# Five projections of the second tile moved into the first tile's attention, and one gathered row in six weighed on VectorE

## The chip, the cores and the metric

The kernel runs on one core of one Trainium2 chip. The metric is the device time of one execution in microseconds. Of the kernel before, three runs gave 1480.18, 1478.48 and 1479.16 us, median 1479.16 us.

## The reference, cut to what matters

256 tokens of width 1024 go through two blocks in float32. The first (projections, a short convolution, a gated delta rule, a convolutional feed-forward) is not touched. The second block works on two tiles of 128 tokens:

```python
# per token: modulated norm, then columns of w_in_2: qa 512 | tok 440 (latent, rope key, index rows) | qb 512 | kb 512 | vb 512 | forget 8
score = sum_h relu(iq_h . ik) * iw_h ; sel = top_k(score, 64)          # branch A: sparse attention over a latent
p_a   = softmax(where(selected and causal, q_lat . latent + q_rope . k_rope))
p_b   = softmax(causal(qb . kb * scale + cum_q - cum_k))               # branch B: forgetting attention
x = x + gate1 * (concat(norm(o_a), norm(o_b)) @ w_out)
h2 = modulated_norm(x)
for head in range(8):                                                   # product keys: 16 of 128 x 128 experts
    expert, g = top16(q1 . keys1, q2 . keys2)
wgt = softmax(g) * gelu(h2 . u[expert])                                 # 128 experts for each token
x = x + gate2 * sum_k wgt_k * v[expert_k]
```

Rows u and v of an expert (1024 numbers each) lie beside each other in HBM, 8 KB together.

## The kernel before

Every engine has its program written out by hand, and semaphores join them. The second block starts where L1033 stands: TensorE ends the feed-forward of the first, and then does tile 0's projections, attention, output projection and expert queries without anything beside them (L1049 to L1130). Tile 1 of the block shares its weights, but is computed later.

**Gathers.** A set is one expert for each of a tile's 128 tokens: one indirect DMA (L2397, GpSimd) brings 128 rows of 8 KB, 1.05 MB, to a slot of SBUF. There are 256 sets, 128 for a tile. `GATHER` says which slot each set takes and which set had it before; there are 7 slots, three more from set 82 and two more from set 116 (`JOIN`). For each set VectorE multiplies the u half by h2 and sums (L2215, "the dot"), ScalarE takes the gelu (L1431), GpSimd lays the weights on a diagonal (L2369), and TensorE multiplies the diagonal by the v half into two PSUM banks (L1027, four instructions of the trace a set). GpSimd may issue the next gather into a slot when TensorE has used it (L2396). The first gather needs the experts of tile 0's first head, which VectorE finds in 17 steps (`route`, L2101 to L2163).

**Ticks.** All of tile 1's work runs between the sets. `until(tick)` on an engine first does that engine's part of the sets up to the tick (TensorE up to tick - 2, ScalarE tick - 1), so the order on each engine is fixed by numbers: tile 1's index rows at tick 3, its projections from tick 6 to 31, its attention from tick 32 on in steps of 4 ticks (`att_tick`), its output projection from 76 (`T_WOUT`), its expert queries from 93 (`T_QUERY`).

**Weights.** Blocks of 2 MB stream through three buffers `wr`, each loaded by SyncE as soon as the block that had the buffer is used: in this part tok, qb, kb, qa, vb, two of w_out, two of w_peer_q (`weight_blocks`). The gathers take over these buffers, so tile 1 can't use the same weights later: they are loaded a second time, in 18 pieces of 0.9 or 1 MB, two at a time in two buffers of their own (`piece`, L531): pieces 0 and 1 before the block starts, each other as the piece two before it is used. TensorE waits for them in `landed_piece`. Tile 1's tok projection (L865) is the one that already stands ahead of the gathers, between tile 0's output projection (L1099, L1104) and the transposes of its expert input (L848).

PSUM banks 0 to 3 go round in the order of the table in `pair_table`; a step waits until the bank of its turn is empty (`claim_bank`). Each engine is in order: what waits holds back all behind it.

Lines that the prediction names: L857, L865 and L881 projections; L890 forget logits; L898 and L848 transposes; L908 index scores; L949 attention logits; L1099 and L1104 output projection of tile 0; L998 expert queries; L2001 and the line behind it one round of the selection of 64 keys; L2022 masks of logits; L1899 in the first block a multiply and add over 1024 columns by VectorE.

## Time and profile before

| | us |
|---|---|
| median of three runs | 1479.16 |
| the profiled execution | 1486.33 |
| its span | 1484.4 |
| PE (TensorE) busy | 1354.0 |
| DVE (VectorE) busy | 841.1 |
| POOL (GpSimd) busy | 429.6 |
| ACT (ScalarE) busy | 292.7 |
| moved by DMA | 424.52 MB, mean 286 GB/s |
| of these by the gathers' queue | 268.48 MB |

The page's chain that ended last gives PE 54%, DMA 26%, issue 7%, POOL 7% of the span. A chain is followed back from the end: where it runs over a DMA, the gather's landing was what came last. Busy times are averages over stages with different limits, so the rows below are cut by stage. In a timeline row the columns are: start and duration in us, engine, line, instruction, what it writes and reads, shape, count; in brackets how long the engine sat idle before it and what ended that.

### The profile page before, as it was taken

How to read it: one execution, taken by the hardware profiler on the slowest of the kernel's cores; microseconds unless marked ns; L12 is line 12 of the kernel's file. 1: busy time of each engine (PE TensorE's matmuls, PEld its weight loads, DVE VectorE, ACT ScalarE, POOL GpSimd, SP SyncE). 2: the span in 40 equal slices, each digit the busy share in tenths (PEclk: the TensorE clock that was granted, in tenths of full speed). 3: DMA queues.
4: the chain of work that ended last, by engine and by line, in shares of the span. 5: the costliest groups of instructions: out<-in, count | busy, mean ns of one | idle time of the engine just before them, and what ended most of it. 6: DMA issues, size and time to landing. Idle time of an engine off the chain costs nothing.

```text
span 1484.4 us, 14879 instructions
## 1 busy us (share of the span) xinstructions
PE 1354.0 (91%) x5314; PEld 872.2 (59%) x5314; DVE 841.1 (57%) x1997; ACT 292.7 (20%) x690; POOL 429.6 (29%) x545
## 2 busy tenths in 40 slices
PE   7999999999999999999988989998989778778776
PEld 6887888898767777667566554444543222222222
DVE  3558451235127667524256567776766767666654
ACT  2023101031010000114423214541221112111101
POOL 0002000120101000000004544564557555655551
PEclk9999999999999999999898998999999999999999
DMA  8343633311557888537339998999999999999995
GB/s 293 115 170 114 227 114 113 120 51 57 171 186 282 309 297 293 204 127 284 113 114 364 423 422 332 395 421 424 424 424 425 425 425 425 425 426 424 425 425 229
DMA packets 119193, 424.52 MB, mean 286 GB/s; under 512 B 10642, under 2 KB 34632, under 8 KB 84176
## 3 DMA queue, kind: packets, MB, share of 16 engines
q0 software_dynamic: 36896, 268.48, 43.7%
q1 hardware_dynamic: 82224, 155.09, 29.0%
q8 instruction: 43, 0.70, 0.2%
q14 instruction: 30, 0.25, 0.0%
HBM read 422.48 MB, written 1.06 MB: 285 GB/s over the span
## 4 chain that ended last, share of the span: by engine, by line
PE 54%; DMA 26%; issue 7%; POOL 7%; ACT 3%; DVE 3%; SPq 0%; POOLq 0%; DVEq 0%; ACTq 0%
PE psum L560 30%; DMA arena<-peer_uv,arena 15%; DMA wr<-peer_uv,arena 7%; PE psum L811 4%; PE psum L1027 3%; POOL wr L2397 3%; POOL arena L2369 2%; DMA xc<-peer_uv,arena 2%; PE psum L787 2%; PE psum L881 1%; PE psum L857 1%; POOL arena L2397 1%; PE psum L608 1%; PE psum L998 1%; PE psum L1045 1%
## 5 line engine op out<-in xcount | busy, mean ns | idle before, releaser
L560 PE MATMUL psum<-hT,wr 128*128 128x256 f32 x1792 | 393.6, 382 | 1.6 <-DVE hT L1583 1.6
L560 PEld LDWEIGHTS psum<-hT,wr 128*128 128x128 f32 x1792 | 342.3, 191 | 51.9 <-issue 5.3
L1027 PE MATMUL psum<-wr,arena 128*128 128x512 f32 x644 | 312.2, 616 | 54.0 <-POOL arena L2369 53.8
L2215 DVE CUSTOM_DVE_ANT_0 wr<-psum,wr 128x1024 f32<-128x1024 f32 x161 | 196.9, 1223 | 148.4 <-DMA wr<-peer_uv,arena 148.3
L1027 PEld LDWEIGHTS psum<-wr,arena 128*128 128x128 f32 x644 | 114.1, 193 | 232.5 <-issue 232.1
L2397 POOL DMA_INDIRECT wr<-peer_uv,arena x161 | 160.8, 999 | 270.0 <-DVE arena L2163 125.4
L1027 PE MATMUL psum<-arena 128*128 128x512 f32 x276 | 135.3, 617 | 27.3 <-POOL arena L2369 27.0
L2369 POOL TENSOR_SCALAR arena<-cst,arena 128x128 f32<-128x128 f32 x256 | 121.8, 476 | 124.7 <-ACT arena L1431 117.1
L1431 ACT ACTIVATE arena<-arena 128x1 f32<-128x1 f32 x256 | 51.0, 202 | 492.8 <-DVE arena L2215 492.3
L1027 PEld LDWEIGHTS psum<-arena 128*128 128x128 f32 x276 | 48.0, 192 | 112.6 <-issue 112.4
L2215 DVE CUSTOM_DVE_ANT_0 arena<-psum,arena 128x1024 f32<-128x1024 f32 x69 | 84.5, 1224 | 50.2 <-DMA arena<-peer_uv,arena 50.1
L1596 DVE TENSOR_SCALAR arena<-psum,vec 128x256 f32<-128x256 f32 x68 | 29.8, 480 | 113.6 <-PE psum L560 105.6
L2356 POOL TENSOR_TENSOR arena<-arena 128x512 f32<-128x512 f32 x11 | 16.9, 1536 | 229.7 <-DVE arena L1598 229.7
L1878 DVE SCALAR_TENSOR_TENSOR arena<-arena,csil 128x512 f32<-128x512 f32 x96 | 78.9, 825 | 3.0
L2397 POOL DMA_INDIRECT arena<-peer_uv,arena x69 | 68.5, 992 | 30.3 <-PE psum L1027 16.2
L1598 DVE SCALAR_TENSOR_TENSOR arena<-psum,vec,arena 128x255 f32<-128x255 f32 (+1 forms) x160 | 69.8, 478 | 2.8
L2344 POOL TENSOR_TENSOR arena<-arena,xc 128x512 f32<-128x512 f32 x12 | 17.0, 1457 | 167.6 <-PE psum L710 133.7
L1027 PE MATMUL psum<-xc,arena 128*128 128x512 f32 x104 | 51.2, 615 | 11.0 <-POOL arena L2369 11.0
L811 PE MATMUL psum<-wr,arena 128*128 128x512 f32 x128 | 55.6, 592 | 0.0
L560 PE MATMUL psum<-arena,wr 128*128 128x256 f32 x256 | 55.4, 379 | 0.0
L560 PEld LDWEIGHTS psum<-arena,wr 128*128 128x128 f32 x256 | 48.6, 190 | 7.0 <-issue 0.5
L1321 ACT ACTIVATE arena<-arena 128x512 f32<-128x512 f32 x11 | 6.9, 630 | 190.1 <-DVE arena L1598 190.1
(321 smaller groups left out, 1458.7 us busy)
## 6 DMA issues: line engine op xcount, KB each, us to landing
wr<-in_w_in SPq DMA_DIRECT2D x22, 2048.0 KB, 8.4
arena<-in_w_ada SPq DMA_DIRECT2D x12, 2048.0 KB, 9.8
wr<-in_w_up SPq DMA_DIRECT2D x22, 1024.0 KB, 8.0
arena<-piece SPq DMA_DIRECT2D x16, 1024.0 KB, 9.1
wr<-in_w_down SPq DMA_DIRECT2D x5, 2048.0 KB, 9.2
wr<-in_w_a_out SPq DMA_DIRECT2D x2, 2048.0 KB, 8.1
wr<-in_w_b_out SPq DMA_DIRECT2D x2, 2048.0 KB, 8.3
wr<-in_w_o SPq DMA_DIRECT2D x2, 2048.0 KB, 7.7
```

What stands on the lines that cost most here:

```text
L560: mm = nc.tensor.matmul(bank[p % 4][:, f * S:(f + 1) * S], slot(i)[:, k, c:c + P], act[:, k, :], start=k == 0, stop=k == KT - 1)
L787: mm = nc.tensor.matmul(bank[4 + 2 * n + t][:, :], sgb[:, k, t * P:(t + 1) * P], slot(23 + n)[:, k, :], start=k == 0, stop=k == KT - 1)
L811: mm = nc.tensor.matmul(bank[4 + 2 * n + t][:, :], act_ffn[:, f, t * P:(t + 1) * P], slot(i)[:, row, n * BANK:(n + 1) * BANK], start=f == ...
L1027: mm = nc.tensor.matmul(bank[(6, 0)[t] + half][:, :], diag[:, n % DIAGS, :], gring[slot_of][:, D + half * BANK:D + (half + 1) * BANK], sta ...
L1431: A_(col, dots[:, t, c:c + 1], ACT.Gelu).then_inc(s["gelu_done"], 1)
L1596: ins = V.tensor_scalar(dst[:, n, :], src[:, n, :], w, None, ALU.mult)
L1598: ins = V.scalar_tensor_tensor(out=dst[:, n, back:S], in0=src[:, n, 0:S - back], scalar=w, in1=dst[:, n, back:S], op0=ALU.mult, op1=ALU.add)
L1878: ins = V.scalar_tensor_tensor(out=part, in0=ada[j % 2][:, k, :], scalar=csil[:, k:k + 1], in1=part, op0=ALU.mult, op1=ALU.add)
L2215: V.tensor_tensor_reduce(gring[slot_of][:, 0:D], h2[t], gring[slot_of][:, 0:D], 1.0, 0.0, ALU.mult, ALU.add, dots[:, t, c:c + 1]).then_inc ...
L2344: G.tensor_tensor(Loff[:, 4 * g:4 * g + 4, :], LT[:, 4 * g:4 * g + 4, :], off, ALU.mult).then_inc(s["loff_done"], 1)
L2369: G.tensor_scalar(diag[:, n % DIAGS, :], ident, wgt[:, t, c:c + 1], gsoft[:, t, c:c + 1], ALU.mult, ALU.mult).then_inc(s["diag_done"], 1)
L2397: G.indirect_dma_start(gring[slot_of], None, A["peer_uv"], bass.IndirectOffsetOnAxis(ap=eid[:, t, c:c + 1], axis=0)).then_inc(g_in[slot_of ...
```

## The change

Three things are changed together.

1. **Tile 1's projections.** The transposes of tile 1's rows (h1a, h1b) and its tok projection move up to tile 0's index scores; the two halves of qb and kb, qa and the two halves of vb of tile 1 stand between the steps of tile 0's attention and use tile 0's weight blocks while they are there. A block is so held until tile 1 has used it too. Ten of the 18 pieces (tok, qb, kb, qa, vb) are not loaded any more; the eight of w_out and w_peer_q stay. Tile 1's index rows, forget logits and first two index scores come ahead of the first gather.
2. **The ticks.** Tile 1's attention starts at tick 16 in steps of 5 ticks (before: 32, steps of 4). The output projection starts at tick 70, the queries at 92, both in steps of 4. Three slots join at set 74 (before 82), two at 118 (before 116).
3. **Sixteen weighted sums.** Sets 8, 14, ..., 98 of tile 0 get no diagonal and no TensorE product. VectorE multiplies the two weights of the set, and adds weight times row to a buffer of its own, behind the dot of the set three later; GpSimd waits for that before it fills the slot again. Ahead of tile 0's end the buffer is added to the PSUM banks (`add_rows`).

The rows of ones that picked a head for the forget logits (`C_SEL`) give way to one column of the identity, read 128 times; that frees SBUF for the buffer.

```diff
-T_TURN, T_WOUT, T_QUERY = 74, 76, 93
+T_TURN, T_WOUT, T_QUERY = 68, 70, 92
 def att_tick(step):
-    return 32 + 4 * step
+    return 16 + 5 * step
-JOIN = {SLOTS: 1, 82: 3, 116: 2}
+JOIN = {SLOTS: 1, 74: 3, 118: 2}
+ON_VECTOR = tuple(range(8, 104, 6))
+def on_tensor(n):
+    return n - sum(m < n for m in ON_VECTOR)
...
-    until("qb", w2[:, :, 952:1464], BANK, "pair_ready", PAIR["qb0b"][0] + 1)
+    until("qb", w2[:, :, 952:1464], BANK, "pair_ready", PAIR["qb1b"][0] + 1)
...
-PIECE_FROM = [("w_in_2", 512, 220), ("w_in_2", 732, 220)]
-PIECE_FROM += [("w_in_2", c + h, 256) for c in (952, 1464, 0, 1976) for h in (0, 256)]
-PIECE_FROM += [(w, c, 256) for w in ("w_out_2", "w_peer_q_2") for c in range(0, D, 256)]
+PIECE_FROM = [(w, c, 256) for w in ("w_out_2", "w_peer_q_2") for c in range(0, D, 256)]
...
             index_rows(0)
+            turn("h1a", 1, 0, 6)
+            turn("h1b", 1, 4, 6)
             by_feature(0, "qb", 1)
             for j in range(4):
                 index_scores(0, j)
+            by_token(1, "tok", 0, 440)
...
-            by_token(0, "qa", 256)
+            by_feature(1, "qb", 0)
             logits(0, 2)
             turned(0, 0)
+            by_token(0, "qa", 0, 512)
...
-            until(28)
-            by_token(1, "vb", 256, 31)
             for step in range(UNITS + 2):
                 until(att_tick(step))
...
+            def vector_sum(n):
+                t, c = divmod(n, P)
+                dve.wait_ge(s["gelu_done"], n + 1)
+                chain(V.tensor_tensor(row_weight[:, :], wgt[:, t, c:c + 1], gsoft[:, t, c:c + 1], ALU.mult))
+                row = gring[GATHER[n][0]][:, D:2 * D]
+                i = ON_VECTOR.index(n)
+                if i == 0:
+                    V.tensor_scalar(row_sum[:, :], row, row_weight[:, 0:1], None, ALU.mult).then_inc(s["row_used"], 1)
+                else:
+                    V.scalar_tensor_tensor(out=row_sum[:, :], in0=row, scalar=row_weight[:, 0:1], in1=row_sum[:, :],
+                                           op0=ALU.mult, op1=ALU.add).then_inc(s["row_used"], 1)
...
                     V.tensor_tensor_reduce(gring[slot_of][:, 0:D], h2[t], gring[slot_of][:, 0:D], 1.0, 0.0, ALU.mult, ALU.add,
                                            dots[:, t, c:c + 1]).then_inc(s["dot_done"], 1)
+                    if n - 3 in ON_VECTOR:
+                        vector_sum(n - 3)
...
-                if before is not None:
-                    pool.wait_ge(s["pe_used"], before + 1)
+                if before in ON_VECTOR:
+                    pool.wait_ge(s["row_used"], ON_VECTOR.index(before) + 1)
+                elif before is not None:
+                    pool.wait_ge(s["pe_used"], on_tensor(before) + 1)
```

Three places show how rows move. First TensorE in tile 0's attention, from the transposes of its weights to the projection vb of tile 0. Before (L964 and L916 transposes, L857 the projection):

```order
L964 MATMUL psum<-cst,arena 128x128 x4
L916 MATMUL psum<-cst,arena 128x128 x4
L964 MATMUL psum<-cst,arena 128x128 x2
L857 MATMUL psum<-wr,hT 128x512 x8
L949 MATMUL psum<-arena 128x128 x2
```

With the change (L957 and L908 are those transposes, L862 the projection, L873 a half of qb or kb):

```order
L957 MATMUL psum<-cst,arena 128x128 x2
L873 MATMUL psum<-hT,wr 128x128 x16
L957 MATMUL psum<-cst,arena 128x128 x2
L908 MATMUL psum<-cst,arena 128x128 x4
L957 MATMUL psum<-cst,arena 128x128 x2
L873 MATMUL psum<-hT,wr 128x128 x16
L862 MATMUL psum<-wr,hT 128x512 x8
L942 MATMUL psum<-arena 128x128 x2
```

The first L873 is tile 1's last use of block qb, and vb loads into the buffer that it frees. The second (tile 1's first half of kb) is all that stands between the two besides ten small transposes.

Second TensorE from the end of tile 0's attention to its expert queries. Before (L984 attention over values, L1099 and L1104 output projection, L865 tok of tile 1, L1117 queries):

```order
L984 MATMUL psum<-arena 128x64 x4
L848 MATMUL psum<-cst,xc 128x128 x12
L1099 MATMUL psum<-wr,hT 128x512 x8
L848 MATMUL psum<-cst,xc 128x128 x4
L1104 MATMUL psum<-wr,hT 128x512 x8
L865 MATMUL psum<-arena,hT 128x220 x16
L848 MATMUL psum<-cst,xc 128x128 x8
L1117 MATMUL psum<-hT,wr 128x128 x16
```

With the change (L862 128x256 the halves of vb of tile 1, L1104 and L1109 the output projection, L890, L882 and L900 index rows, forget logits and two index scores of tile 1, L1123 queries):

```order
L862 MATMUL psum<-wr,hT 128x256 x8
L977 MATMUL psum<-arena 128x64 x2
L854 MATMUL psum<-cst,xc 128x128 x4
L862 MATMUL psum<-wr,hT 128x256 x8
L1104 MATMUL psum<-wr,hT 128x512 x8
L854 MATMUL psum<-cst,xc 128x128 x4
L1109 MATMUL psum<-wr,hT 128x512 x8
L890 MATMUL psum<-cst,arena 128x128 x4
L882 MATMUL psum<-hT,fbw 8x128 x8
L900 MATMUL psum<-arena 128x256 x4
L854 MATMUL psum<-cst,xc 128x128 x8
L1123 MATMUL psum<-hT,wr 128x128 x16
```

The tok projection is gone from behind the output projection, smaller steps stand there, and two halves of vb stand ahead of it.

Third VectorE at the dots of sets 16 and 17. Before (L2215 and ISA the dot, L1980 and L1982 index sums of tile 1, L2148 and L2152 steps of `route`):

```order
L2148 TENSOR_TENSOR arena<-arena,cst 128x256 x2
L2215 ISA wr,arena<-psum,wr 128x1024
L2215 ISA arena 128x1
L1980 TENSOR_SCALAR arena<-arena,iws 128x256
L1982 SCALAR_TENSOR_TENSOR arena<-arena,iws 128x256
L2152 TENSOR_TENSOR arena<-arena 128x256 x2
L2215 ISA wr,arena<-psum,wr 128x1024
```

With the change (L2226 the dot, L2158 and L2162 steps of `route`, L2048 and L2056 the sum of set 14, L2008 a mask of tile 1's first logits):

```order
L2158 TENSOR_TENSOR arena<-arena,cst 128x256 x2
L2226 ISA wr,arena<-psum,wr 128x1024
L2226 ISA arena 128x1
L2162 TENSOR_TENSOR arena<-arena 128x256 x2
L2226 ISA wr,arena<-psum,wr 128x1024
L2226 ISA arena 128x1
L2048 TENSOR_TENSOR row_weight<-arena 128x1
L2056 SCALAR_TENSOR_TENSOR row_sum<-wr,row_weight,row_sum 128x1024
L2008 ISA arena,amax<-psum,cst 128x256
```

The index sums have moved ahead to sets 6 to 12, and attention and a weighted sum stand where they stood.

## Rows read from the trace of the kernel before

**Rows 1.** Stages by time: busy us of each engine, PE clock, DMA share, GB/s.

```profile
669.00:757.00 88.00, 83.96 (x394) 54.17 (x393) 30.54 (x124) 31.04 (x90) 0.00 (x0) 0.92 0.49 178
779.00:804.00 25.00, 20.72 (x101) 14.77 (x101) 19.01 (x67) 9.58 (x21) 11.88 (x15) 0.82 0.90 335
804.00:892.00 88.00, 82.94 (x339) 50.23 (x337) 53.41 (x142) 14.68 (x45) 40.83 (x54) 0.99 1.01 421
892.00:944.00 52.00, 50.87 (x146) 23.07 (x144) 38.42 (x118) 25.36 (x52) 25.24 (x34) 0.92 0.91 338
944.00:1110.00 166.00, 150.82 (x544) 81.04 (x544) 114.75 (x309) 53.56 (x131) 90.18 (x121) 0.99 1.01 423
1110.00:1473.00 363.00, 288.50 (x592) 101.47 (x591) 239.25 (x596) 55.56 (x174) 209.35 (x289) 0.99 0.99 417
```

**Rows 2.** The chain that ended last, a piece: start us, us, what.

```profile
1188.94 25.77 DMA arena<-peer_uv,arena
```

**Rows 3.** Timeline of PE, 678 to 763, and index scores at 822.

```profile
678.44 1.91 PE L890 MATMUL psum<-hT,fbw 128*8 128x128 f32 x16
...
689.77 7.41 PE L881 MATMUL psum<-hT,wr 128*128 128x128 f32 x64
...
700.97 7.13 PE L857 MATMUL psum<-wr,hT 128*128 128x512 f32 x16
...
716.48 8.57 PE L857 MATMUL psum<-wr,hT 128*128 128x512 f32 x16
...
738.44 9.61 PE L1099 MATMUL psum<-wr,hT 128*128 128x512 f32 x16 [1.23 <-ACT hT L1329]
...
756.25 6.11 PE L865 MATMUL psum<-arena,hT 128*128 128x220 f32 x32
...
762.19 1.06 PE L848 MATMUL psum<-cst,xc 128*128 128x128 f32 x8
...
822.28 1.14 PE L908 MATMUL psum<-arena 32*128 32x256 f32 x8
```

**Rows 4.** DMA issues, 779 to 1473 and 640 to 800: KB, us to landing.

```profile
arena<-piece SPq DMA_DIRECT2D x14, 1024.0 KB, 9.2
...
wr<-in_w_out SPq DMA_DIRECT2D x2, 2048.0 KB, 8.1
```

**Rows 5.** Timeline of DVE: tile 0's expert input and first routing.

```profile
761.85 0.69 DVE L2075 TENSOR_TENSOR xc<-xc,arena 128x512 f32<-128x512 f32 x1
...
768.88 0.49 DVE L2101 MAX8 arena<-arena 128x8 f32<-128x128 f32 x2 [2.61 <-ACT arena L1343]
...
777.89 0.17 DVE L2163 CAST arena<-arena 128x16 uint32<-128x16 f32 x1
```

**Rows 6.** Timeline of POOL: gathers 0, 4 and 7.

```profile
778.96 1.05 POOL L2397 DMA_INDIRECT wr<-peer_uv,arena  x1 [125.36 <-DVE arena L2163]
...
790.31 0.93 POOL L2397 DMA_INDIRECT wr<-peer_uv,arena  x1 [6.57 <-PE psum L998]
...
798.11 1.00 POOL L2397 DMA_INDIRECT wr<-peer_uv,arena  x1 [3.43 <-PE psum L1027]
```

**Rows 7.** Timeline of PE where tile 1's attention starts.

```profile
888.92 0.67 PE L949 MATMUL psum<-arena 64*128 64x256 f32 x2 [3.54 <-ACT arena L1343]
```

**Rows 8.** DVE by line, 860 to 1460; behind it L1899 in the timeline.

```profile
L2215 DVE CUSTOM_DVE_ANT_0 wr<-psum,wr 128x1024 f32<-128x1024 f32 x135 | 165.1, 1223 | 118.7 <-DMA wr<-peer_uv,arena 118.5
...
L2001 DVE MAX8 top<-arena 128x8 f32<-128x256 f32 x8 | 3.4, 424 | 0.0
...
664.18 1.28 DVE L1899 SCALAR_TENSOR_TENSOR x<-x,stat,arena 128x1024 f32<-128x1024 f32 x1
```

**Rows 9.** The page's diagonals; one in the timeline, and DVE beside it.

```profile
L2369 POOL TENSOR_SCALAR arena<-cst,arena 128x128 f32<-128x128 f32 x256 | 121.8, 476 | 124.7 <-ACT arena L1431 117.1
...
833.21 1.18 POOL L2369 TENSOR_SCALAR arena<-cst,arena 128x128 f32<-128x128 f32 x1 [0.84 <-ACT arena L1431]
...
833.02 0.47 DVE L1968 TENSOR_TENSOR_SCAN small<-cst,small 8x128 f32<-8x128 f32 x1
```

More of the change, by code:

```diff
@@ L69, in constant_table @@
         t[:, C_NEG + n * S:C_NEG + (n + 1) * S] = np.where(seen, 0.0, -BIG)
-    for h in range(H):
-        t[h, C_SEL + h * P:C_SEL + (h + 1) * P] = 1.0
     t[:, C_IOTA:C_IOTA + 16] = np.arange(16)
@@ L849, in turn, with by_token @@
                 mm.then_inc(s["pair_ready"], 1)
[L851 to L868 removed]
+            def by_token(t, name, first, cols, claimed=None):
+                o = claim_bank(claimed or f"{name}{t}")
+                weights(at[name])
+                for k in range(KT):
+                    mm = nc.tensor.matmul(o[:, 0:cols], hT[:, k, tiles_of[t]], slot(at[name])[:, k, first:first + cols],
+                                          start=k == 0, stop=k == KT - 1)
                 mm.then_inc(s["pair_ready"], 1)
@@ L1050, in _ @@
             emptied(pe, "h0b")
-            by_token(0, "tok", 220)
+            by_token(0, "tok", 0, 440)
             forget(0)
@@ L1060, in _ @@
                 index_scores(0, j)
+            emptied(pe, "h1a")
+            emptied(pe, "h1b")
+            by_token(1, "tok", 0, 440)
             by_feature(0, "kb", 0)
@@ L1105, in _ @@
                 mm.then_inc(s["wout_ready"], 1)
-            emptied(pe, "h1a")
-            emptied(pe, "h1b")
-            by_token(1, "tok", 220)
+            index_rows(1)
+            forget(1)
+            index_scores(1, 0)
+            index_scores(1, 1)
             turn("g0a", 0, 0, 9)
```

206 lines of the change are left out of this document (94 added, 112 removed), and 4 rows, old and new, of the table names.

## The prediction, made before the changed kernel ran

> **What bounds the kernel now.** I read the stages first [rows 1]. From 804 us on the DMA share is 0.99 to 1.01 in all stages but one, and the rate 421 to 423 GB/s: the gathers fill the DMA engines. The chain of waits says the same: it runs over one gather after another, 25.77 us from issue to landing in the row shown [rows 2]. So behind 779 us time is bytes by rate, plus what the stages of lower rate lose. Two lose: 779 to 804 moves 335 GB/s, which against 423 is 25 x (1 - 335/423) = 5.2 us, and 892 to 944 moves 338 GB/s, 52 x (1 - 338/423) = 10.4 us. The last stage up to 1473 moves 417 on average because it contains the run-out after the last gather.
>
> Ahead of 779 us the bound is another: TensorE is busy 83.96 of 88 us from 669 to 757 [rows 1], and its steps follow on each other with hardly a gap [rows 3]. Then comes a chain that no other work shortens: the output projection (its last products end where L865 starts, 756.25), x and the norm on VectorE until 761.85 + 0.69 = 762.54, the queries, and the routing of the first head, 768.88 to 778.06 [rows 3, 5]. The first gather leaves at 778.96 [rows 6]. The change lays TensorE work from the second regime, where it was hidden, into the first, where it is not, and takes bytes and TensorE work out of the second.
>
> **Ahead of the first gather.** Added to tile 0's attention: the two halves of qb and of kb, each pair 7.41 us (L881 x64), 14.8; qa 7.13; the two halves of vb together as many columns as vb of tile 0, 7.13 [rows 3]. That is 29.1 us. The tok projection, 6.11 us, was already in this stretch, but it was free where it stood: it ended at 762.2, when VectorE was just through with the expert input at 762.54. What stands there now (forget logits 1.91, two index scores 1.14, four transposes) is shorter, and TensorE waits for VectorE instead, so the transposes L848 come no earlier after the output projection than before. At its new place tok costs its 6.1 us. Together 35.2. The clock and the waits are counted apart:
>
> - A new wait. Block vb can load only when tile 1's second half of qb has been used. Between the two TensorE has 3.7 us of kb and about 1.3 us of transposes (the first fence of the change); a 2 MB block takes 8.1 us from issue to landing [rows 4]. That leaves 3.1 us of waiting. The same for qa (behind tok) is covered: 7.4 of kb, logits and 3.7 of qb lie between.
> - Old waits that go. TensorE idles 4.0 us of the 88 in the stage; 1.23 of it before L1099, which a half of vb now covers [rows 1, 3]. I take 2.0 of the 4.0.
> - The clock. The same vb and output steps that take 7.13 us at the 2.4 GHz level take 8.57 (716.48) and 9.61 (738.44) in the trace; both follow stretches of waits and small transposes, and the granted clock of the stage is 0.92 [rows 1, 3]. At most 88 x 0.08 = 7 us can come back. Long projections now stand between the small steps, which speaks for it; the new wait before vb and the one before L848 speak against. Ends 0 and 7; I take 4, just above the 3.9 of the two long steps.
>
> By the Trainium skill ("TensorE: Matmul & The Clock Gate", What's actually happening) the low clock is the default state and activity releases it. By that rule alone the denser stream would win back the whole 7 us, and the stage would cost 3 us less than I say; the trace agrees that the low level follows thin work, but the two new waits are of the kind that it punishes.
>
> Sum: 35.2 + 3.1 - 2.0 - 4.0 = 32.3 us later for the first gather (ends 29 and 36).
>
> **Behind the first gather.**
>
> - Bytes. 14 pieces load there now [rows 4], 6 with the change (pieces 0 and 1 of the eight are loaded ahead). 8 x 1.049 MB / 423 GB/s = 2.48 us each: 19.8 us less. These are bytes on the bound, so this is the safest term.
> - Start. Gathers 4 to 6 leave only at 790.31, 11.3 us behind the first, since they wait for the last query projection, which stood behind the forget logits and its emptying by VectorE; gather 7 leaves at 798.11, when TensorE has done the first sum [rows 6]. The forget logits now stand ahead. Of the 5.2 us about 2 are the way from issue to full rate and stay; I take 3.0 back (ends 0 and 3.5).
> - Tile 1's attention. Its first logits wait 3.54 us for ScalarE to empty vb1, which stands behind 33 gelus on ScalarE [rows 7]; there the ring falls behind, the clock falls to 0.92, and steps of 4 ticks (9.9 us of gathers) hold more work of TensorE than 9.9 us. All of this goes: vb1 is emptied before the gathers, a step has 5 ticks (12.4 us), and one sum in six is off TensorE. So I take back the 10.4 us, and put against it what is new:
> - VectorE becomes the tight engine. A set costs it a dot, 1.22 [rows 8], and a sixteenth of a head's routing, 9.2 / 16 = 0.57 [rows 5]: 1.8 of 2.47 us. With the attention at ticks 16 to 31 come two rounds of selection (0.42 each for two passes, 1.7 for two rounds) and a mask in two passes of the same width (about 0.85) for five sets, 0.5 a set; and a weighted sum, 1.28 by L1899, the same operation on the same 1024 columns, with its small multiply about 1.5 for six sets, 0.25 a set [rows 8]. That makes 2.55 to 2.6 of 2.47. The sets 6 to 15 are as full: index sums, the mask of scores and the turning of the queries, which before had until set 31, stand there. Over these 26 sets VectorE falls 3 to 5 us behind.
> - The slots. A slot of a VectorE set comes free three landings later and after dot and sum: 7.4 + 2.8 = 10.2 us behind its landing. With 7 slots the next gather must start 14.8 us behind it and needs about 2 us from issue: 2 to 3 us to spare, less than VectorE's lag. GpSimd, in order, holds the following diagonals and gathers while it waits. Nothing of this counts after set 74, where there are 10 slots.
>
> Together I put 5 us of new loss (ends 0, if the ring absorbs the lag, and 15, if each of the 11 sums before set 74 costs the 1.28 us of its operation once on the bound).
>
> The 16 sums themselves take 16 x 1.8 us off TensorE, which isn't the bound there, and add 24 us to VectorE, which has 0.6 us to spare in most sets: nothing by themselves. Adding the buffer to PSUM (two steps over 512 columns) stands at set 164, under 12 slots: nothing. The run-out after the last gather is unchanged.
>
> **Sum.** 32.3 - 19.8 - 3.0 - 10.4 + 5.0 = +4.1 us. On the profiled execution, 1486.33, that is 1490.4; the median of the runs is 7.2 us below that execution, and the same step from 1479.16 gives 1483.3. I say 1483.
>
> **The rivals.**
>
> 1. *Everything is recovered: faster.* The clock holds (first gather 29 later), and the ring absorbs VectorE's lag (new loss about 1): 29 - 19.8 - 3.0 - 10.4 + 1 = -3.2, 1476 us. For it: the lag is near what 7 slots have to spare, and DMA ran at 421 GB/s beside a TensorE busy 94% of the time from 804 to 892 [rows 1]. Against: the new wait of 3.1 us for vb. It decides if new losses stay under 1.5 us and the clock of the stage is 0.98 or more.
> 2. *The parts cancel.* One of the two holds and not the other: -1 to +2, about 1479.5.
> 3. *VectorE holds the ring.* The release behind the dot three sets later, with VectorE late, starves the gathers at each of the 11 sums: 12 us of new loss instead of 5, +11, 1490. For it: a diagonal took 1.18 us instead of 0.476 on average when VectorE had instructions with two inputs in SBUF beside it [rows 9], so that a sum can also hold GpSimd up to 1.28 us, on the engine that issues gathers. Against: an issue late by that much costs nothing while other gathers are under way. The Trainium skill ("SBUF — State Buffer", SBUF: two separate sides) has it as a rule: a VectorE instruction with two SBUF inputs and a GpSimd instruction that reads SBUF exclude each other for their whole length. By it the sixteen sums, of which the first has one input, cost GpSimd up to 15 x 1.28 = 19 us in all, an estimate with the row's 1.28, and the time would move only as far as that meets the ring.
> 4. *It doesn't do what it says*: a bank or buffer held longer stops TensorE in tile 0's attention. I found no such turn in the table of banks.
>
> **How the numbers follow.** About 0.2% (3 us) is what a measurement of this kernel can tell from no change. My forecast (+1 to +7): 0.40, of which 0.28 lies over +3 and 0.12 within. Rival 1: 0.27, 0.23 of it under -3 and 0.04 within. Rival 2: 0.18, all within. Rival 3: 0.13, slower. Rival 4: 0.02, half on each side. Faster 0.24, same 0.34, slower 0.42. The forecast's own range is 1480 to 1486; the range for 8 in 10 takes in most of rivals 1 and 3: 1473.5 to 1491.
>
> **What the profile of the changed kernel would show.** The first gather at about 811 us (808 to 815); L862 vb of tile 0 behind a wait of about 3 us for a DMA into wr; a granted clock of 0.95 or more in tile 0's attention. Six pieces behind the first gather. Gathers 0 to 6 within 9 us. No wait of TensorE for ScalarE at the start of tile 1's attention. In the stretch 30 to 80 us behind the first gather a rate under 420 GB/s with GpSimd waiting for VectorE's sums. Wrong I am if the first gather comes before 806 or after 816, or if the stretch from first gather to last isn't 25 to 32 us shorter.

## The result and the profile after

The changed kernel takes 1505.4 us (median of 1506.28, 1505.99, 1499.46 and 1504.82) against 1479.67 for the kernel before (median of four); ratio 1.0142, 95% interval 1.0122 to 1.0161. It is slower by 21 to 26 us, where 4 were forecast. The profiled execution is 1506.28, its span 1504.5.

The gathers first (counted from 0): gathers 0, 6 and 7; gathers 21 and 26, which fill the slots of sets 14 and 19; and the last (POOL in the timeline; columns as in [rows 6]).

```profile
811.91 1.05 POOL L2414 DMA_INDIRECT wr<-peer_uv,arena  x1 [160.42 <-DVE arena L2173]
819.49 0.94 POOL L2414 DMA_INDIRECT xc<-peer_uv,arena  x1 [0.30 <-ACT arena L1421]
828.37 1.00 POOL L2414 DMA_INDIRECT wr<-peer_uv,arena  x1 [3.74 <-PE psum L1022]
864.21 0.99 POOL L2414 DMA_INDIRECT wr<-peer_uv,arena  x1 [3.64 <-DVE row_sum L2056]
880.53 1.00 POOL L2414 DMA_INDIRECT wr<-peer_uv,arena  x1 [7.61 <-PE psum L1022]
1468.25 0.99 POOL L2414 DMA_INDIRECT wr<-peer_uv,arena  x1 [0.20 <-issue]
```

The first leaves at 811.91 against 778.96 [rows 6]. From the first gather to the last it is 656.3 us (called the first-to-last stretch below); before, the last left at 1447.80, so 668.8. The forecast wanted this stretch 25 to 32 us shorter, and it is 12.5 shorter. That is where the forecast broke.

Stages of the changed kernel: ahead of the first gather, gathers 0 to 7, 20 to 31, 32 to 43, 44 to 79, 80 to 103 (columns as in [rows 1]).

```profile
670.00:812.00 142.00, 132.04 (x732) 96.13 (x731) 46.14 (x191) 43.65 (x121) 0.09 (x1) 0.95 0.34 119
812.00:831.00 19.00, 10.80 (x48) 6.63 (x47) 14.78 (x53) 4.75 (x12) 8.93 (x11) 0.73 0.92 365
859.00:899.00 40.00, 33.40 (x84) 14.51 (x83) 34.20 (x99) 18.22 (x38) 16.86 (x23) 0.83 0.91 354
899.00:935.00 36.00, 31.89 (x79) 15.15 (x80) 24.38 (x71) 13.30 (x28) 16.98 (x23) 0.81 0.88 329
935.00:1024.00 89.00, 68.54 (x202) 33.32 (x201) 69.41 (x184) 29.19 (x72) 50.17 (x65) 0.94 0.99 392
1024.00:1098.00 74.00, 58.60 (x209) 33.47 (x208) 53.84 (x125) 14.49 (x39) 35.90 (x45) 0.93 1.01 425
```

Behind set 80 the DMA engines are full, as before. The new hole is at 859 to 935: 354 and 329 GB/s, with a granted clock of 0.83 and 0.81. Against 423 that is 40 x (1 - 354/423) + 36 x (1 - 329/423) = 14.5 us. The dip of the kernel before (the stage of 338 GB/s [rows 1]) cost 10.4; it did not go, it moved ahead with the attention and grew. Sets 44 to 79 behind it lose another 89 x (1 - 392/423) = 6.5 us, where the kernel before was at the full rate from 944 us on. In the hole TensorE is busy for 65.3 of 76 us.

TensorE ahead of the first gather (timeline): a half of qb, the projection vb of tile 0, a half of vb of tile 1, the output projection, the first queries.

```profile
705.95 5.47 PE L873 MATMUL psum<-hT,wr 128*128 128x128 f32 x32
736.46 8.80 PE L862 MATMUL psum<-wr,hT 128*128 128x512 f32 x16 [3.46 <-DMA wr<-in_w_in]
768.05 3.62 PE L862 MATMUL psum<-wr,hT 128*128 128x256 f32 x16
771.51 7.03 PE L1104 MATMUL psum<-wr,hT 128*128 128x512 f32 x16
779.76 7.13 PE L1109 MATMUL psum<-wr,hT 128*128 128x512 f32 x16 [0.78 <-DVE hT L2040]
795.08 5.78 PE L1123 MATMUL psum<-hT,wr 128*128 128x128 f32 x32 [0.83 <-issue]
```

The wait for vb is there (3.46). The output projection rose to the high level (7.03 for 9.61 [rows 3]); vb of tile 0 stayed low (8.80 for 8.57 [rows 3]); and the half of qb (5.47 against 3.62 for as many columns at 768.05) and the first queries (5.78, in the kernel before 3.81) run partly at the low level, the first behind eight small steps of logits, the second behind transposes and waits. So the clock was won in one place and lost in two.

### The profile page after: what moved, and what is told of

It is laid out like the page before. It is cut to its first block, busy times and chain, and to the rows that moved or that the text cites. A ratio compares the mean times of both kernels' runs of the same rounds, so it can differ in the third digit from the quotient of the medians.

```text
span 1504.5 us, 14703 instructions
## 1 busy us (share of the span) xinstructions
PE 1336.2 (89%) x5218; PEld 859.9 (57%) x5218; DVE 862.2 (57%) x2031; ACT 291.8 (19%) x689; POOL 424.8 (28%) x529
## 4 chain that ended last, share of the span: by engine, by line
PE 54%; DMA 26%; issue 7%; POOL 6%; DVE 4%; ACT 1%; POOLq 0%; SPq 0%; DVEq 0%; ACTq 0%
PE psum L566 30%; DMA wr<-peer_uv,arena 12%; DMA arena<-peer_uv,arena 11%; PE psum L817 4%; PE psum L1022 3%; POOL wr L2414 3%; PE psum L862 2%; POOL arena L2384 2%; PE psum L793 2%; PE psum L873 2%; DMA xc<-peer_uv,arena 2%; DMA wr<-in_w_in 1%; PE psum L614 1%; PE psum L1040 1%; POOL arena L2414 1%
## 5 line engine op out<-in xcount | busy, mean ns | idle before, releaser
L1022 PE MATMUL psum<-wr,arena 128*128 128x512 f32 x584 | 294.2, 637 | 85.4 <-POOL arena L2384 85.2
L1022 PEld LDWEIGHTS psum<-wr,arena 128*128 128x128 f32 x584 | 107.8, 201 | 257.6 <-issue 257.1
L2226 DVE CUSTOM_DVE_ANT_0 wr<-psum,wr 128x1024 f32<-128x1024 f32 x158 | 193.0, 1221 | 107.0 <-DMA wr<-peer_uv,arena 106.6
L1022 PE MATMUL psum<-arena 128*128 128x512 f32 x280 | 137.1, 616 | 35.4 <-POOL arena L2384 35.1
L2384 POOL TENSOR_SCALAR arena<-cst,arena 128x128 f32<-128x128 f32 x240 | 115.9, 483 | 118.6 <-ACT arena L1421 108.3
L2226 DVE CUSTOM_DVE_ANT_0 arena<-psum,arena 128x1024 f32<-128x1024 f32 x72 | 88.1, 1224 | 59.6 <-DMA arena<-peer_uv,arena 59.5
L2414 POOL DMA_INDIRECT arena<-peer_uv,arena x72 | 72.5, 1007 | 34.0 <-PE psum L1022 13.4
L817 PE MATMUL psum<-wr,arena 128*128 128x512 f32 x128 | 55.6, 592 | 0.0
L862 PE MATMUL psum<-wr,hT 128*128 128x512 f32 (+2 forms) x112 | 42.4, 534 | 3.5 <-DMA wr<-in_w_in 3.5
```

Source lines behind the costliest of these rows:

```text
L817: mm = nc.tensor.matmul(bank[4 + 2 * n + t][:, :], act_ffn[:, f, t * P:(t + 1) * P], slot(i)[:, row, n * BANK:(n + 1) * BANK], start=f == ...
L862: mm = nc.tensor.matmul(o[:, 0:cols], hT[:, k, tiles_of[t]], slot(at[name])[:, k, first:first + cols], start=k == 0, stop=k == KT - 1)
L1022: mm = nc.tensor.matmul(bank[(6, 0)[t] + half][:, :], diag[:, on_tensor(n) % DIAGS, :], gring[slot_of][:, D + half * BANK:D + (half + 1) * ...
L2226: V.tensor_tensor_reduce(gring[slot_of][:, 0:D], h2[t], gring[slot_of][:, 0:D], 1.0, 0.0, ALU.mult, ALU.add, dots[:, t, c:c + 1]).then_inc ...
L2384: G.tensor_scalar(diag[:, i % DIAGS, :], ident, wgt[:, t, c:c + 1], gsoft[:, t, c:c + 1], ALU.mult, ALU.mult).then_inc(s["diag_done"], 1)
L2414: G.indirect_dma_start(gring[slot_of], None, A["peer_uv"], bass.IndirectOffsetOnAxis(ap=eid[:, t, c:c + 1], axis=0)).then_inc(g_in[slot_of ...
```

## The experiments

Ratios are against the kernel before, each with its 95% interval. The five comparisons gave that kernel medians of 1481.0 to 1483.9 us. Each profile is of one execution.

The expectations weigh five theories. A: VectorE has more to do than it has time for. B: a slot that comes free behind VectorE's sum holds GpSimd, and all that GpSimd does next. C: TensorE's clock falls and its sums come late. D: a step of tile 1's attention holds more TensorE work than its gathers take. E: not the amount but the lump of that work delays the ring of slots.

### The three parts apart

The changed kernel without VectorE's sums:

```
-ON_VECTOR = tuple(range(8, 104, 6))
+ON_VECTOR = ()
```

> The changed kernel with all sums back on TensorE (no set on VectorE), attention at ticks 16 + 5 x step as changed. The stretch from first gather to last landing is 20 us longer than forecast in the changed kernel. Theory A (VectorE overfull: attention packed early plus sums): about half of the 20 us returns, 1495. Theory B (the release of the slots behind VectorE's sums, with GpSimd held in order): nearly all returns, 1486 to 1488. Theory C (TensorE's clock falls and its sums come late, whoever does the other sums): little returns, 1500 to 1505.

Measured: 1495.54 us, 1.0095 (1.0062 to 1.0129).

Only the projections moved: as above, and all ticks back:

```
-    return 16 + 5 * step
+    return 32 + 4 * step
-T_TURN, T_WOUT, T_QUERY = 68, 70, 92
+T_TURN, T_WOUT, T_QUERY = 74, 76, 93
...
```

> Only the projections moved: no sum on VectorE, and tile 1's index sums, selection, attention (32 + 4 x step), output projection, queries and slots at the ticks of the kernel before. Ahead of the first gather +35 as in the changed kernel, 8 pieces less is -20, the start -3. Theory A: the ring has no new loss, 1479.7 + 12 minus what the dip at the start of tile 1's attention gives back (up to 10): 1482 to 1490, some 5 to 10 below the run without sums. Theory B: the same as the run without sums, within 2. Theory C: within 3 of the changed kernel's 1505 less what the start gives.

Measured: 1497.33 us, 1.0099 (1.0067 to 1.0130).

Sums, but the ticks back: the second edit without the first.

> The changed kernel with its 16 sums on VectorE, but with tile 1's index sums, selection, attention and what follows at the ticks of the kernel before. Theory A: VectorE has room for the sums then; 1485 to 1492, at least 12 below the changed kernel. Theory B: the sums cost as before, 1498 to 1505. Together with the two other runs this gives a square: sums yes or no, early or late.

Measured: 1501.44 us, 1.0131 (1.0089 to 1.0174).

The kernel before with the sums only (and, for their buffer, the forget logits' ones from the identity's column):

```
+ON_VECTOR = tuple(range(8, 104, 6))
...
```

> The kernel before with the 16 sums on VectorE and nothing else (the row of ones for the forget logits gives way to the identity's column, as in the change). Theory A: VectorE has room around its other work; within 3 us of the kernel before. Theory B: 11 sums ahead of set 74 hold the ring about 1.3 us each, +8 to +14. Neither: a gain of some us at 892 to 944, where TensorE was late and has six sums less to do.

Measured: 1487.48 us, 1.0028 (1.0004 to 1.0053).

So the projections alone make +0.99%, 14.7 us, two thirds of the loss. The sums cost 0.28%, 0.32% and 0.47% (4 to 7 us) on the three bases. Moving the ticks brings 0.04% without sums and costs 0.11% with them. The intervals of single runs are about 0.3% wide on each side, so the last two are not told from zero, and neither is the 0.47% quite (1.0129 and 1.0122 are the ends that meet). The 0.28% is (its interval starts at 1.0004), and so is the 0.32%: on one chip five executions took 1496.10 to 1498.23 us without the sums and four took 1501.31 to 1503.07 with them. Of the ticks it is told that most of the 10.4 us (0.7%) of the forecast did not come. One profile speaks for a part of it: that of the run without sums is the fastest of its five executions (1489.71), and its first-to-last stretch (810.97 to 1451.68) is 28.1 us shorter than before, 5.1 more than that of the run with the old ticks. By the medians the two differ by 1.8 us, and two kernels below that differ little from it (steps of six, steps cut in two) have 645.9 and 645.4, as long as with the old ticks. Its sets 20 to 43 still are below the full rate:

```profile
857.00:893.00 36.00, 33.75 (x93) 14.58 (x92) 30.34 (x94) 17.86 (x37) 17.61 (x24) 0.95 0.99 390
893.00:922.00 29.00, 27.91 (x85) 12.56 (x84) 22.18 (x66) 13.29 (x28) 18.05 (x25) 1.00 0.98 390
```

The stretch between first and last gather of the run with only the projections moved (814.34 and 1460.16) is 645.8, 23.0 shorter than before: the 19.8 of bytes and a rest of 3.2, most of which gather 7 shows (it leaves 16.7 behind the first instead of 19.2); and its dip, two stages of sets 32 to 55, is that of the kernel before:

```profile
891.00:927.00 36.00, 29.70 (x73) 12.38 (x72) 30.33 (x94) 13.91 (x31) 17.95 (x24) 0.91 0.91 368
927.00:962.00 35.00, 33.99 (x106) 16.57 (x107) 24.95 (x70) 15.20 (x33) 18.52 (x25) 0.95 0.95 354
```

### How a sum on VectorE reaches the gathers

The diagonals of the two sets behind laid ahead of the wait:

```
-                while before is not None and laid <= before + 1:
+                while before is not None and laid <= before + (3 if before in ON_VECTOR else 1):
```

> The changed kernel (1.0142 of the kernel before). Where a gather waits for a sum of VectorE, GpSimd now lays the diagonals of the two sets behind first; nothing else differs. In the trace of the changed kernel GpSimd waits for L2056 up to 3.6 us with the next diagonals behind it, TensorE then idles for the diagonal, and its granted clock is 0.81 to 0.83 in sets 20 to 44. Theory B (GpSimd held in order starves TensorE, which falls to 1.2 GHz and can't catch up): most of the 7 to 10 us that the sums cost returns, ratio 1.008 to 1.011, clock of sets 20 to 44 at 0.93 or more. Theory A (VectorE itself is overfull): within 0.2% of the changed kernel.

Measured: 1499.56 us, 1.0105 (1.0076 to 1.0135).

Zeros added where TensorE skips a set:

```
                     if n in ON_VECTOR:
+                        for half in range(2):
+                            nc.tensor.matmul(bank[6 + half][:, :], cst[:, C_NEG + S:C_NEG + S + P], cst[:, 0:BANK], start=False, stop=False)
                         continue
```

> The changed kernel with TensorE also adding zeros to the two banks (two products over 512 columns, as long as one set's) where it skips a VectorE set; they wait for nothing. Theory C (the idle gap of a skipped set lowers the clock): the granted clock goes back to 0.98 of the run without sums and the time to 1.009 to 1.011. Theory B or A: TensorE has 16 x 1.88 us more to do at the places where it was already late, the waits stay: 1.013 to 1.020.

Measured: 1500.8 us, 1.0120 (1.0087 to 1.0152).

Both edits:

> The changed kernel (1.0142) with both edits: diagonals of the two sets behind laid ahead of a wait for VectorE's sum (1.0105 alone), and zeros added by TensorE in place of the skipped sets (1.0120 alone). Theories B and C together say that the sums' price is the held diagonals and the clock, so that with both it goes to that of the kernel without sums, 1.0085 to 1.0105. Theory A leaves 2 to 4 us for VectorE's own time: 1.011 to 1.013.

Measured: 1499.38 us, 1.0107 (1.0074 to 1.0140).

The chain can be read in the changed kernel. GpSimd and VectorE around one sum, then TensorE (timeline):

```profile
862.65 1.28 DVE L2056 SCALAR_TENSOR_TENSOR row_sum<-wr,row_weight,row_sum 128x1024 f32<-128x1024 f32 x1
865.25 0.45 POOL L2384 TENSOR_SCALAR arena<-cst,arena 128x128 f32<-128x128 f32 x1
865.84 3.67 PE L1022 MATMUL psum<-wr,arena 128*128 128x512 f32 x8 [2.63 <-POOL arena L2384]
875.76 1.09 PE L957 MATMUL psum<-cst,arena 128*128 128x128 f32 x4 [0.71 <-DVE amax L2008]
876.64 3.62 PE L1022 MATMUL psum<-wr,arena 128*128 128x512 f32 x4
...
900.81 2.97 PE L1022 MATMUL psum<-xc,arena 128*128 128x512 f32 x4 [2.96 <-POOL arena L2384]
...
917.77 2.86 PE L1022 MATMUL psum<-wr,arena 128*128 128x512 f32 x4 [2.00 <-POOL arena L2384]
```

The gather at 864.21 waits 3.64 for the sum at 862.65; the diagonal of the next set stands behind that gather; TensorE idles 2.63 for the diagonal. Ten us on, one set takes 3.62 (876.64) instead of 1.96: the low level, 1.2 GHz. The next gather then waits 7.61 for TensorE (880.53). So a part of the sums' price is not VectorE's 1.28 us, but the order on GpSimd, which carries a wait for VectorE over to TensorE. Laying the diagonals ahead takes 0.37% back of 0.47%; all four intervals overlap, so the share is not sharp. The filler adds 30 us of TensorE work and does not slow the kernel (1.0120 against 1.0142), with the granted clock of the profiled execution back from 0.971 to 0.979. The profiles, over the same two stretches behind the first gather, have neither edit bring all of it back (the profile without sums is the fastest of its executions, that with the diagonals ahead the slowest):

| | 47 to 87 us: GB/s, clock | 87 to 123 us: GB/s, clock | first to last gather, us |
|---|---|---|---|
| changed kernel | 354, 0.83 | 329, 0.81 | 656.3 |
| diagonals ahead | 359, 0.87 | 370, 0.95 | 653.8 |
| zeros | 375, 0.96 | 379, 0.95 | 648.6 |
| both | 359, 0.83 | 393, 1.00 | 648.9 |
| without sums | 380, 0.96 | 411, 1.00 | 640.7 |

By the Trainium skill ("TensorE: Matmul & The Clock Gate", HAM oscillation — how this bites in real kernels) waits between bursts throttle the engine again and again. The rows agree in part. From 859 to 935 us the granted clock falls three times, at 874.3, 901.6 and 918.7. The last two falls come within one us of the end of idle times of 2.96 (900.81) and 2.00 (917.77), but the first, which lasts longest (to 888.0), comes 8.5 us behind the end of the idle time of 2.63, with TensorE busy but for 0.19 us between. That a wait for a diagonal lowered the clock there is not shown.

### What bounds the attention's stretch

Steps of six ticks (without sums):

```
-    return 16 + 5 * step
+    return 16 + 6 * step
```

> The changed kernel without VectorE's sums (1.0095) and with tile 1's attention in steps of 6 ticks instead of 5, what follows it 9 ticks later and in steps of 3. Theory D: TensorE is the bound of the attention's stretch. A step has 2.8 us of logits, 0.6 of transposes and 1.0 of products with values, 4.4 in all, and 5 sums of 1.88 us: 13.8 against 5 x 2.48 = 12.4 of bytes. With 6 sets 15.7 against 14.9: less is lost in each step, though over more sets; the total of the stretch falls short by 0.8 x 10 instead of 1.4 x 10, some 5 us better, 1.006. If VectorE or the fixed order bound it: within 0.2% of 1.0095.

Measured: 1496.58 us, 1.0096 (1.0069 to 1.0123). The 5 us did not come.

Each step cut in two (without sums):

```
                 if step == 1:
                     queries_a(1)
+                until(att_tick(step) + 2)
```

> The changed kernel without VectorE's sums (1.0095), with each step of tile 1's attention on TensorE cut in two: the logits at tick t, the transposes and the products with values at t + 2 with two sums between. Theory E: not the amount of TensorE work (steps of 6 changed nothing) but its lump delays the ring: 4.4 us in one piece hold the sums back by more than the 2 us that 7 slots spare. In pieces of 2.8 and 1.6 us: sets 20 to 44 rise from 390 to 410 GB/s or more, ratio 1.005 to 1.007. Otherwise: within 0.2% of 1.0095.

Measured: 1494.81 us, 1.0082 (1.0049 to 1.0114), not told from 1.0095. Sets 20 to 43 move 402 and 386 GB/s, so the lump is not the cause of what is lost there.

One slot less (without sums):

```
-JOIN = {SLOTS: 1, 74: 3, 118: 2}
+JOIN = {74: 3, 118: 2}
```

> The changed kernel without VectorE's sums (1.0095) with 6 slots instead of 7 up to set 74. It gives the price of ring depth. Theory E (the ring has 2 us to spare with 7 slots and stalls come from lumps longer than that): 6 slots take 2.5 us of slack away, so that nearly every tick of sets 8 to 74 with any other work loses: +10 to +25 us, 1.016 to 1.026. If throughput of an engine bound those stages, depth would matter little: under 1.013.

Measured: 1507.44 us, 1.0174 (1.0140 to 1.0207).

Half of the sums' columns, on the changed kernel without sums on VectorE:

```
-                    for half in range(2):
+                    for half in range(1 if 14 <= n < 70 else 2):
```

> The changed kernel without VectorE's sums (1.0095); for sets 14 to 69 TensorE does only the first half of the columns, 0.94 us less a set. The second half of tile 0's output lacks these experts. Theory D (TensorE is the bound of tile 1's attention, 13.8 us of work for 12.4 of bytes): the stretches under 420 GB/s at sets 20 to 70 go, 5 to 9 us, ratio 1.004 to 1.006. Theory A (VectorE is the bound there): within 0.2% of 1.0095.

Measured: 1492.08 us, 1.0065 (1.0039 to 1.0090).

The same on the kernel before, for sets 30 to 75:

> The kernel before; for sets 30 to 75 TensorE does only the first half of the columns. The second half of tile 0's output lacks these experts. Theory D: the stage of 338 GB/s (10.4 us lost by the prediction) was TensorE's, 11.9 us of work in a step of 9.9: it goes but for the wait of 3.5 us for ScalarE, ratio 0.994 to 0.996. If VectorE's lateness (0.42 us masks, routing, dots) makes it: 0.998 or more.

Measured: 1478.72 us, 0.9970 (0.9956 to 0.9983).

Without six rounds of selection:

```
                     until(att_tick(unit) + 3)
-                    take_round(1)
                     until(att_tick(unit) + 4)
-                    take_round(1)
```

> The changed kernel without VectorE's sums (1.0095), without the six rounds of tile 1's selection that stand between the steps of its attention (so the selection holds 16 of 64 keys), 0.85 us of VectorE each for sets 19 to 30. Theory A (VectorE, with routing, dots, masks and rounds, is the bound of sets 20 to 32): the loss of 390 GB/s there goes, 3 us, ratio 1.0075 or less. Theory D: within 0.15% of 1.0095.

Measured: 1493.84 us, 1.0086 (1.0054 to 1.0118).

Halving the products gives 0.30% on both kernels (4.4 us), taking 5 us of VectorE away gives 0.09%, not told from nothing. Only on the kernel before is the 0.30% clear of noise; on the changed kernel the two intervals overlap, and the profiles show no gain: 398 GB/s from 860 to 937 against 395 over the same time without the edit (380 and 411 in the table above), first-to-last stretches of 640.9 and 640.7. In the kernel before the sets 32 to 55 then read:

```profile
869.00:908.00 39.00, 32.80 (x88) 15.58 (x87) 30.03 (x89) 14.09 (x31) 17.25 (x24) 0.87 0.99 399
908.00:940.00 32.00, 28.19 (x97) 14.21 (x97) 24.42 (x69) 14.98 (x33) 18.12 (x26) 0.89 0.99 385
```

Against 423 that is a loss of 5.1 us. Its first-to-last stretch is 662.2 (777.52 to 1439.74), 6.6 us shorter, 1.3 of it by gather 7 at the start. So about half of the dip of the kernel before was TensorE's, which there is busy for 50.87 of 52 us [rows 1] and has more to do than the gathers give it time for. A step of the attention in the changed kernel without sums, TensorE in the timeline, from one step's first logits to the next's:

```profile
884.83 0.70 PE L942 MATMUL psum<-arena 64*128 64x256 f32 x2
885.45 0.69 PE L945 MATMUL psum<-small,cst 8*128 8x256 f32 x2
...
887.32 0.66 PE L957 MATMUL psum<-cst,arena 128*128 128x128 f32 x4
887.82 1.00 PE L977 MATMUL psum<-arena 128*128 128x64 f32 x8
888.66 3.65 PE L1022 MATMUL psum<-wr,arena 128*128 128x512 f32 x8
...
898.33 0.70 PE L942 MATMUL psum<-arena 64*128 64x256 f32 x2
```

From 884.83 to 898.33 it is 13.5 us for five sets, whose bytes take 5 x 2.48 = 12.4. TensorE idles 0.5 us in it. So the first four of the eight steps are too short at 5 ticks too; at 4, with one set of 1.95 less, it is 11.6 for 9.9. The other four have no L945 and fit into 12.4. By this count the dip would be 4 x 1.1 = 4.4 us at 5 ticks, where the profile loses 5.1, and at 4 ticks 4 x 1.7 with the wait of 3.54 [rows 7] 10.3, where it lost 10.4 (estimates from these rows). At 6 ticks it is 15.5 for 14.9, only 2 us better than at 5, which those runs could not have told from nothing: the 5 us expected of them counted all steps as long. Less depth costs 11.7 us by the ratios: with 6 slots the ring spares less, and more of every lateness is lost. In the run with 6 slots sets 20 to 31 fell to this:

```profile
864.00:900.00 36.00, 31.79 (x86) 13.92 (x85) 25.88 (x84) 16.66 (x35) 17.40 (x24) 0.90 0.84 319
```

### The attention on the kernel before, with sums only there

```
+ON_VECTOR = tuple(range(36, 84, 5))
-    return 32 + 4 * step
+    return 32 + 9 * step // 2
...
```

> The kernel before with its projections where they were; tile 1's attention in steps of 4.5 ticks (end at 72 instead of 68, what follows 4 or 2 later), sums on VectorE only at sets 36, 41, ... 81, where TensorE is the late engine, and the diagonals behind them laid ahead of the wait. Theory D with B: the stage of 338 GB/s (10.4 us lost) gets back half or more, ratio 0.994 to 0.998. Theory A: the ten sums cost VectorE what they save TensorE, within 0.2% of the kernel before or slower up to 1.004.

Measured: 1489.37 us, 1.0033 (1.0016 to 1.0051). In its sets 68 to 79 the clock is 0.83 at 369 GB/s, where the kernel before has 422 at 1.00. Nor did the dip give back its half: gathers 36 to 43 and 44 to 55 move 360 and 353 GB/s (886 to 914 and 914 to 950 us), where the kernel before moves 351 and 352 (886 to 914 and 914 to 948).

### The start of the gathers

The forget logits behind the queries:

```
-            forget(1)
             for j in range(1, 4):
                 peer_queries(0, j)
                 key_scores(0, j)
+            forget(1)
```

> The kernel before, with tile 1's forget logits (L890) taken from between the first and the second query projection of tile 0 to behind the last key scores, and nothing else. In the trace before, gather 4 leaves 11.3 us behind the first since it waits for the last query projection, which waits for a bank that VectorE empties behind the first routing. Forecast by the start term of the prediction (3.0 us, ends 0 and 3.5): gathers 4 to 6 leave within 9 us of the first, ratio 0.998 (0.9975 to 1.000).

Measured: 1485.76 us, 1.0024 (1.0009 to 1.0039). Slower, though the first gather left at 776.45 and gather 6 at 784.02. VectorE, GpSimd's first diagonals and TensorE's first sum in its timeline:

```profile
783.00 0.34 DVE L1954 TENSOR_SCALAR small<-psum,gate_par 8x128 f32<-8x128 f32 x1 [7.46 <-PE psum L890]
793.85 0.89 POOL L2369 TENSOR_SCALAR arena<-cst,arena 128x128 f32<-128x128 f32 x2 [8.89 <-DVE arena L2177]
794.45 3.75 PE L1027 MATMUL psum<-wr,arena 128*128 128x512 f32 x4 [11.48 <-POOL arena L2369]
```

Seven gathers fill the seven slots; the eighth needs a sum, that a diagonal, that head 0's softmax on VectorE, behind the dot of set 1. So that was moved:

```
-                    if n == LAG:
+                    if n == 0:
                         for step in range(3):
                             softmax_sum(0, step)
...
                 route(0, step)
+            until(4)
             forget_logits(1)
```

> The kernel before with three moves. TensorE's forget logits of tile 1 behind tile 0's last key scores (as in the run that was 1.0024), VectorE's part of them behind the dot of set 3, and the sum, reciprocal and product of head 0's softmax ahead of dot 0 instead of behind dot 1. In the run with TensorE's part moved alone gathers 0 to 6 left within 7.6 us, but VectorE waited 7.46 us for L890, and the first diagonal came at 793.85 as in the kernel before, behind L2177. If the first diagonal is the bound of the start, TensorE's first sum starts at 787 to 789 instead of 794.4 and gather 7 leaves at 791 instead of 798: 3 to 6 us, ratio 0.996 to 0.998. If the start is bound by the way from issue to landing: within 0.2% of the kernel before.

Measured: 1481.14 us, 0.9987 (0.9973 to 1.0000). The timeline has:

```profile
786.56 3.40 PE L1027 MATMUL psum<-wr,arena 128*128 128x512 f32 x4 [2.63 <-POOL arena L2370]
790.24 1.01 POOL L2398 DMA_INDIRECT wr<-peer_uv,arena  x1 [1.53 <-PE psum L1027]
802.78 0.72 POOL L2370 TENSOR_SCALAR arena<-cst,arena 128x128 f32<-128x128 f32 x1 [5.38 <-ACT arena L1431]
```

Almost eight us earlier than in the kernel before for the first sum and gather 7, but then GpSimd waits 5.38 for a gelu, behind four table loads of 1.28 us on ScalarE. ScalarE's part of the forget logits therefore went from tick 6 to tick 15:

```
             until(6)
             copy_index(1)
-            forget(1)
...
+            forget(1)
             copy_relu(0)
```

> The kernel before with the early softmax (0.9987) and ScalarE's part of the forget logits at tick 15 instead of 6. In the run with the early softmax ScalarE loads four function tables for it (L1364, L1366, L1424, L1431, 1.28 us each) while GpSimd waits 5.38 us for a gelu at 802.78, and the gather behind it leaves 7.3 us after the one before. If those tables are what the start still loses: 2 to 3 us more, ratio 0.996 to 0.998. If the loss only moves to tick 15: 0.9987 again.

Measured: 1479.87 us, 0.9975 (0.9965 to 0.9986). This version beats both kernels; 776 to 801 us, its start, moves 388 GB/s where the kernel before has 335 [rows 1]:

```profile
776.00:801.00 25.00, 21.04 (x115) 13.46 (x114) 20.78 (x70) 7.78 (x20) 15.29 (x20) 1.00 0.95 388
```

And the early softmax on the changed kernel without sums:

> The changed kernel without VectorE's sums (1.0095) and with head 0's softmax ahead of dot 0. In the changed kernel the first diagonal comes at 823.74 behind L2187, 11.8 us behind the first gather, and gather 7 leaves 16.5 us behind it; in the kernel before with the early softmax gather 7 left 12.8 us behind. The same here is 3 to 4 us in the start: ratio 1.006 to 1.0075, so that of the changed design without the sums some 9 to 11 us stay, which is what the first gather comes later (35) less the bytes (20) and less the start. If the ring gives it back later: 1.0095.

Measured: 1496.41 us, 1.0097 (1.0074 to 1.0120), nothing. Gather 7 leaves at 822.52, 13.2 behind the first instead of 15.6, and it is given back at once to the same table loads (gather 11 leaves 25.3 behind the first, for 25.4):

```profile
833.94 0.45 POOL L2383 TENSOR_SCALAR arena<-cst,arena 128x128 f32<-128x128 f32 x1 [4.17 <-ACT arena L1421]
```

## Why the prediction was wrong

The sign was right, the size was not: +4.1 forecast, +21 by the ratio. By its steps:

- **Added TensorE work, 35.2, and the new wait, 3.1.** Right: the added steps take 37 us in the trace, of which the slow half of qb has 1.8, and the wait is 3.46.
- **The clock, 4.0 back, and old waits, 2.0.** Mis-sized. From tok to the first gather it is 141.6 us against 106.5, so 35.1 where I said 32.3: on balance hardly anything of the clock came back, as one long step rose to the high level and two fell. The other profiles agree: with these two, seven of kernels with the same program ahead of the gathers as the kernel before, or nearly so, have the first gather at 775.57 to 779.64, thirteen of the changed design at 809.15 to 814.58, 35 apart in the mean.
- **Bytes, -19.8, and the start, -3.0.** Right as a sum: 23.0 with the projections alone. The start's mechanism was half right. Gathers 4 to 6 left early, but what bounds gather 7 is the first diagonal, and moving only the queries gave nothing.
- **The dip, -10.4.** This is the step that failed: "All of this goes". The runs show, in its place, that moving the ticks was worth 0.04%, 0.6 us (at best 5 us by one profile), and that the changed kernel loses 14.5 us there. I had the reason in hand, more TensorE work in a step than a step's gathers last, and did not do the sum for the new step: 13.5 us for 12.4 of bytes without VectorE's sums. I took the wait of 3.54 for ScalarE [rows 7] and the short step for the whole cause. With one sum in six off TensorE, as in the changed kernel, the same step would take 13.5 - 5/6 x 1.88 = 11.9 us (an estimate from the rows of the step above) and fit. So there the work alone isn't the cause. Of the 76 us from 859 to 935 TensorE waits for 10.7 and runs at the low level for about 27, worked out from the clocks of 0.83 and 0.81.
- **New loss, +5.0 (ends 0 and 15).** The sums cost 7.0 us on this kernel (1.0142 less 1.0095), inside the ends. I had VectorE's lateness and GpSimd's order, but not what stands between them and the time: TensorE waits for the diagonal and works at 1.2 GHz for a part of the stretch where it has most to do. That the size came out near is in part luck. How the 7.0 us divide between the waits and the clock is not shown.
- **"Off TensorE, which isn't the bound there ... nothing by themselves".** Wrong in both halves. On the kernel before TensorE bounds half of the dip, by the run with half of the columns; on the changed kernel that run is not clear of noise. And taking sums off it made the kernel slower on each of the three bases.

With the ratios: projections +14.7, ticks -0.6, sums +7.0, together +21.1. The forecast for the same three was +9.5 (32.3 - 19.8 - 3.0), -10.4 and +5.0. So 9.8 of the 17 us missing are the dip, 5.2 the projections (2.8 of it seen ahead of the gathers, the rest within the interval of 4.6 on either side), 2.0 the sums. Rival 3 came nearest, 1490 from the sums holding the ring at 12 us, and it too had the dip recovered. Of its lock rule the trace shows something: of the 14 sums with two inputs that start from 862 to 1089 us four ran beside a diagonal, and these took 0.58, 1.54, 0.58 and 1.34 instead of 0.45:

```profile
935.78 1.54 POOL L2384 TENSOR_SCALAR arena<-cst,arena 128x128 f32<-128x128 f32 x1
935.88 1.28 DVE L2056 SCALAR_TENSOR_TENSOR row_sum<-wr,row_weight,row_sum 128x1024 f32<-128x1024 f32 x1
```

The lock of the Trainium skill ("SBUF — State Buffer", SBUF: two separate sides) is thus seen in part, at 2.2 us in all and not 19. By that page the one that starts first keeps the ports; the diagonal at 935.78 starts 0.10 ahead of the sum by the trace and still takes 1.54, so the order is not as the page has it, or not as the trace shows the starts.

Open stays how much of the dip is left for what else once TensorE is relieved: half the columns brought back 5.3 of 10.4 us by the rates on the kernel before and 4.4 by the ratio. An eighth slot, which would test the depth from the other side, was not tried.

## What to carry to other kernels

Work moved out of a stage bound by bytes costs its full time wherever it lands on the path: 35 us on TensorE here for 20 us of bytes. Before a dip is booked as a gain, add up the suspected engine's work in one step of the new schedule and set it against the bytes of that step; if it is still larger, the dip moves with the work. If it fits, count the waits that the new schedule adds to it. And relieving an engine in an in-order chain by another engine's work adds a wait for that one; look at who issues behind the wait.

## What the hardware showed

- TensorE's clock can be lost by taking work off it: 0.986 in the profile without VectorE's sums, 0.971 with them. Adding 30 us of products with zeros brought it to 0.979 and cost nothing that the runs could see. A lower clock is not a longer time by itself: with half of the columns in sets 30 to 75 the kernel before has 0.974 instead of 0.983 in the profiles and takes 0.9970 of the time.
- The same program has its stage ahead of the gathers at another clock from one execution to the next: from 670 to 760 us 0.92 in the kernel before, with the first gather at 778.96, and 0.98 and 775.57 in the kernel before with the sums, which ahead of the gathers differs from it only in where the forget logits read their ones. Fifteen executions of the kernel before on one chip lay between 1476.41 and 1487.68 us.
- A diagonal of GpSimd beside a VectorE instruction with two inputs in SBUF can take three times as long: 1.54 us for one that starts 0.10 ahead of a sum of 1.28, 1.34 for one that starts 0.77 into such a sum, instead of 0.45. Two others, which met the last quarter of a us of a sum, took 0.58.
